# A one-layer hybrid encoder block on one core: residual update ahead of the last modulation tile, weight splits between operand pairs, roots read from PSUM, latent sums one block later, stores from two queues

## The reference

```
mod = silu(c) @ w_ada + b_ada          # six vectors: shift, scale, gate for mixer and MLP
h = rms_norm(x, norm_mix) * (1 + sc_a) + sh_a
p = h @ w_in                           # 3912 columns, split among three head groups
p_cq, p_ckv, p_kr, p_sb, p_fox, p_f = split(p)
q  = rms_norm(p_cq,  q_norm)  @ w_uq   # latent attention, group A
kv = rms_norm(p_ckv, kv_norm) @ w_ukv
o  = [mla(q, kv, rope(p_kr)), stick_breaking(p_sb), forgetting(p_fox, p_f)], per-head RMSNorm
x = x + g_a * (o @ w_out)
h = rms_norm(x, norm_ffn) * (1 + sc_m) + sh_m
x = x + g_m * (relu(h @ w_ff1) ** 2 @ w_ff2)      # d_ff = 8192
return rms_norm(x, final_norm)
```

## Time and profile before

| | |
|---|---|
| median of three runs | 1131.03 us (1129.48 to 1132.12) |
| the profiled execution, its own time | 1133.37 us |
| its span, first to last instruction | 1131.6 us |
| PE busy | 1098.3 us (97%) |
| DVE, ACT, POOL busy | 719.9, 532.8, 315.1 us |
| mean granted TensorE clock | 0.990 |
| read from HBM | 293.37 MB |

### The profile page before, as it was taken

How to read it: one execution, slowest core, us unless ns; L and a number is a source line. 1 busy time by engine, 2 the same in 40 slices (tenths; PEclk the granted TensorE clock), 3 DMA queues, 4 the chain that set the end, 5 groups by cost and what they waited for, 6 DMA issues and landing times.

```text
span 1131.6 us, 21714 instructions
## 1 busy us (share of the span) xinstructions
PE 1098.3 (97%) x9084; PEld 1065.4 (94%) x9084; DVE 719.9 (64%) x924; ACT 532.8 (47%) x674; POOL 315.1 (28%) x157
## 2 busy tenths in 40 slices
PE   7989999999999999999999999999999999999996
PEld 6879999997799989999999999999999999999995
DVE  4588877888866569877875544545655555444453
ACT  4644454676574445444444434334444544344341
POOL 2998997865049950000000000000000000000001
PEclk8999999999999999999999999999999999999998
DMA  9999999999759858888886665656566656565651
GB/s 348 409 409 403 398 372 371 379 352 330 248 226 408 326 204 314 307 302 284 279 272 195 190 202 189 197 192 191 183 206 196 193 191 201 190 196 189 193 184 75
DMA packets 81888, 296.88 MB, mean 262 GB/s; under 512 B 9088, under 2 KB 9216, under 8 KB 81792
## 3 DMA queue, kind: packets, MB, share of 16 engines
q1 hardware_dynamic: 81792, 295.50, 73.7%
HBM read 293.37 MB, written 2.10 MB: 261 GB/s over the span
## 4 chain that ended last, share of the span: by engine, by line
PE 83%; DMA 5%; DVE 3%; POOL 3%; issue 2%; ACT 1%; SPq 1%; DVEq 0%; ACTq 0%
PE ps L1408 50%; PE ps L1414 25%; DMA ada<-in_ada 3%; POOL w_lo L845 3%; PE ps L1426 2%; DMA raw<-in_weights 2%; PE ps L1595 2%; PE ps L1431 1%; DVE ada L972 1%; SPq L443 0%; POOL ssq L839 0%; PE ps L1605 0%; PE ps L1450 0%; ACT w_hi L493 0%; PE ps L1635 0%
## 5 line engine op out<-in xcount | busy, mean ns | idle before, releaser
L493 ACT ACTIVATE w_hi<-raw 128x1024 fp32r<-128x1024 f32 x338 | 355.3, 1059 | 431.4 <-PE ps L1414 358.2
L953 DVE TENSOR_TENSOR w_lo<-raw,w_hi 128x1024 fp32r<-128x1024 f32 x254 | 308.7, 1224 | 267.3 <-ACT w_hi L493 266.8
L1408 PE MATMUL ps<-hT,w_hi 128*128 128x256 f32 x3072 | 382.8, 277 | 8.3 <-DVEq L1040 3.0
L1408 PEld LDWEIGHTS ps<-hT,w_hi 128*128 128x128 f32 x3072 | 365.3, 189 | 12.0 <-issue 3.9
L1408 PE MATMUL ps<-act,w_hi 128*128 128x256 f32 x2048 | 252.9, 276 | 0.0
L1408 PEld LDWEIGHTS ps<-act,w_hi 128*128 128x128 f32 x2048 | 241.6, 188 | 0.0
L845 POOL TENSOR_TENSOR w_lo<-raw,w_hi 128x1024 fp32r<-128x1024 f32 x84 | 200.6, 2413 | 36.1 <-ACT w_hi L493 35.6
L1414 PE MATMUL ps<-hT,w_lo 128*128 128x256 f32 x1536 | 205.8, 276 | 0.7 <-DVE w_lo L953 0.7
L839 POOL TENSOR_TENSOR ssq<-ssq,sq 128x1024 f32<-128x1024 f32 x6 | 14.4, 2408 | 657.3 <-ACT sq L500 657.3
L1414 PEld LDWEIGHTS ps<-hT,w_lo 128*128 128x128 f32 x1536 | 188.8, 188 | 0.9 <-DVE w_lo L953 0.9
L1414 PE MATMUL ps<-act,w_lo 128*128 128x256 f32 x1024 | 136.9, 276 | 0.0
(11 more groups left out here) (229 smaller groups left out, 833.1 us busy)
## 6 DMA issues: line engine op xcount, KB each, us to landing
raw<-in_weights SPq DMA_DIRECT2D x338, 512.0 KB, 4.4
ada<-in_ada SPq DMA_DIRECT2D x176, 512.0 KB, 6.4
more<-in_weights SPq DMA_DIRECT2D x24, 512.0 KB, 7.6
more<-in_ada SPq DMA_DIRECT2D x16, 512.0 KB, 7.9
xT<-in_xt SPq DMA_DIRECT2D x4, 512.0 KB, 7.3
y<-tmp SPq DMA_DIRECT2D x4, 256.0 KB, 2.5
consts<-in_consts SPq DMA_DIRECT2D x1, 580.0 KB, 12.4
y<-sq SPq DMA_DIRECT2D x2, 256.0 KB, 3.0
```

What stands on the lines that cost most here:

```text
L493: sc.activation(w_hi[:, slot, :, :], raw_room(u0 + j), ACT.Copy).then_inc(hi_done, 1)
L953: ve.tensor_tensor(w_lo[:, slot, :, :], raw_room(u), w_hi[:, slot, :, :].bitcast(F32), ALU.subtract).then_inc(lo_vec, 1)
L1408: pe.matmul(acc[:, n, :], w, rhs[:, kt0 + k, half, :], start=first and k == 0 and n % 2 == 0 and half == 0, stop=False, skip_group_check=True)
```

## The change

Seven edits, in program order.

1. `USE_LST` goes from 37 to 38: PE makes the latents' sums after block 4 of the last part, and DVE's `latent_means` and ACT's `root_latents` move from block 4 to block 5. `lat_operand(1)` no longer follows `root_latents`; `lat_operand(2)` does.
2. DVE does `gate_out(3)` before `ada_tile(159)` and `make_gain`.
3. `rough` for the second norm and the final norm reads the sums in PSUM itself (Ln with scale 1/2048 and epsilon as a bias, a new column of `cols`). DVE's `mean` waits for that Ln, and so runs beside the Exp; `invert` waits for `mean` only at its second instruction.
4. The feed-forward's first unit (`first_unit`) multiplies the high operand half by all of `w_hi`, then `w_lo`, and only then the low half.
5. ACT converts B_FF+4 to B_FF+8 behind operand pairs 3 to 7; it was B_FF+4 and +5 behind pairs 6 and 7.
6. DVE splits B_FF+2 to B_FF+6 among the pairs (in passes 3, 4, 5, 7 and 8 of its loop); it was B_FF+2 and +3 in passes 3 and 4.
7. The three stores of POOL's results are issued by ACT, the five of DVE's by SP.

```
+            def rough(n, use=None, bank=0, ready=0):
+                if use is None:
...
+                else:
+                    sc.wait_ge(psum_ready, ready)
+                    sc.activation(y0[:, 0, :], ps[use % 2][:, bank, 0:S], ACT.Ln, scale=1.0 / D,
+                                  bias=cols[:, C_EPS:C_EPS + 1]).then_inc(ln_step, 1)
...
                 operand_hi(R_FFN + j, ...)
-                if j >= 6:
-                    hi(B_FF + LAG, 0, 0, j - 6)
+                if j >= 3:
+                    hi(B_FF + LAG, 0, 0, j - 3)
...
                 ve.wait_ge(newton, 2 * n - 5)
+                ve.wait_ge(mean_done, n)
...
-                    if last and b == 4:
+                    if last and b == 5:
                         latent_means()
...
-                    ada_tile(a)
+                    if a + 1 < A_GM:
+                        ada_tile(a)
...
+            gate_out(3)
+            ada_tile(A_GM - 1)
             make_gain(SC_M, C_FFN, 0, KT, A_GM - 1)
-            gate_out(3)
             ve.wait_ge(gain_ready, 9)
-            ve.wait_ge(psum_ready, READY_FFN)
+            ve.wait_ge(ln_step, 3)
...
-                if j in (3, 4):
-                    lo(B_FF + j - 1)
+                if j in (3, 4, 5, 7, 8):
+                    lo(B_FF + (3, 4, 5, 7, 8).index(j) + 2)
...
+            for n, k in enumerate((6, 8, 10)):
+                sc.wait_ge(result_pool, n + 1)
+                sc.dma_start(out[:, k * S:(k + 2) * S],
+                             result_tiles(k).rearrange("p a b -> p (a b)")).then_inc(ld_out, 16)
...
-            def unit(u, banks, rhs, kt0, ready, first, last, ahead=None):
+            def first_unit(u, banks):
+                acc = quarters(banks)
+                pe.wait_ge(hi_done, u + 1)
+                for k in range(UK):
+                    pe.wait_ge(*((first_hi, 1), (op_hi, R_FFN + 1))[k])
+                    for n in range(4):
+                        pe.matmul(acc[:, n, :], w_hi[:, u % RING, k, n * P:(n + 1) * P], hT[:, k, 0, :],
...
-                    if p + 1 == len(PARTS) and b == 3:
+                    if p + 1 == len(PARTS) and b == 4:
                         take(USE_LST)
```

More of the change, by code:

```diff
@@ L802, in _ @@
                     for b in range(2):
-                        for j in range(2 if half == it == b == 0 else 0, 8):
+                        for j in range(5 if half == it == b == 0 else 0, 8):
                             hi(base + LAG, 16, it, 8 * b + j)
@@ L1394, in take, with unit @@
                     pe.wait_ge(psum_free, use)
[L1396 removed]
+            def first_unit(u, banks):
[5 more added lines that the diff above has]
+                        pe.matmul(acc[:, n, :], w_hi[:, u % RING, k, n * P:(n + 1) * P], hT[:, k, 0, :],
+                                  start=k == 0 and n % 2 == 0, stop=False, skip_group_check=True)
+                pe.wait_ge(*lo_ready(u))
+                for k in range(UK):
+                    for n in range(4):
+                        pe.matmul(acc[:, n, :], w_lo[:, u % RING, k, n * P:(n + 1) * P], hT[:, k, 0, :],
+                                  start=False, stop=False, skip_group_check=True)
+                for k in range(UK):
+                    pe.wait_ge(*((first_lo, 1), (op_lo, R_FFN + 1))[k])
+                    for n in range(4):
+                        ins = pe.matmul(acc[:, n, :], w_hi[:, u % RING, k, n * P:(n + 1) * P], hT[:, k, 1, :],
+                                        start=False, stop=False, skip_group_check=True)
+                ins.then_inc(unit_used, 1)
+            def unit(u, banks, rhs, kt0, ready, first, last):
                 slot = u % RING
                 acc = quarters(banks)
[L1400 removed]
+                pe.wait_ge(*ready)
                 pe.wait_ge(hi_done, u + 1)
                 for k in range(UK):
[L1403 to L1404 removed]
                     for n in range(4):
```

39 lines of the change are left out of this document (17 added, 22 removed).

## The result

The changed kernel takes 1156.29 us, the median of four runs (1152.78 to 1157.76), against 1131.57 us (1129.48 to 1134.82, four runs) before: a ratio of 1.0212, interval 1.0189 to 1.0235. Forecast were 1124.4. The profiled execution took 1155.15 us, its span is 1153.4, the mean granted clock 0.992 (before 0.990).

A forecast was written before the change was run, and what follows sets the result against it. PE, busy 97% of the span, was taken to bound the kernel. Savings of 2.85 + 0.46 + 0 + 2.79 + 0 + 0.46 + 0.1 = 6.66 us took the median from 1131.03 to 1124.4 us, range 1122.4 to 1126.9.

The forecast's parts named there:

- Update ahead and root from PSUM: Passage into the feed-forward part: residual update first saves 2.85 us, Ln reading PSUM beside `mean` saves 0.46.
- The root term: Second norm's root: Ln reads PSUM at once, `mean` runs beside Exp; 0.46 us saved, bounds 0.46 gain, about 0.4 loss.
- First unit: Feed-forward unit 0: an earlier start only lengthens the stop before unit 1; 0 saved, bounds 0 and 0.1 us.
- Splits: Feed-forward unit 4: earlier splits remove PE's wait for `w_hi` and `w_lo`; 2.79 us saved, bounds 1.3 and 2.79.
- Rival (a): Feed-forward splits stay late: half of 2.79 us remains, 1125.8, or all, 1127.2; chance 0.11.
- Latents: Latents' sums after block 4: slow clock taken to come again, 0 saved; bounds 1.0 us saved, 0.7 lost.
- rival (e): Latents keep the full clock: 1.0 us saved and no slow-clock cost, 1123.4 or a little less; chance 0.05.
- rival (b): Clock falls at the feed-forward part's head, on units 0 to 2, costing 1.24 to 1.7 us: 1125.9; chance 0.06.
- Stores: Kernel's tail: two store queues fill part of the first transfer gap; 0.1 us saved, bounds 0.19 saved, 0.2 lost.

The follow-up runs named there:

- after: The changed kernel with all seven edits: 1156.29 us, median of four runs, ratio 1.0212 to the kernel before.
- a_old_first: Changed kernel with the old order of matmuls in the feed-forward's first unit: 1127.11, 1155.86, 1156.41 and 1157.08 us.
- b_early_splits: Kernel before with only the earlier conversions by ACT and splits by DVE: 1129.82, 1154.81, 1155.55 and 1163.16 us.
- a_late_splits: Changed kernel with the earlier conversions and splits undone: seven runs of 1128.38 to 1132.52 us, three of 1155.38 to 1158.98.
- before: The kernel without the change: 1131.57 us, median of four runs.
- b_set: Kernel before plus a float32 matmul ahead of feed-forward unit 6, an own-type one ahead of unit 10: eight runs 1129.96 to 1134.62 us, four 1159.17 to 1163.30.
- b_slow: Kernel before plus one float32 matmul ahead of feed-forward unit 6: 1132.0, 1157.1, 1160.83 and 1162.34 us.
- a_set: Changed kernel plus a float32 matmul ahead of feed-forward unit 2 and an own-type 128-column one ahead of unit 6: median 1128.45 us, six runs.
- a_own: Changed kernel plus only one own-type 128-column matmul ahead of feed-forward unit 6: 1127.29, 1129.26, 1154.21 and 1154.95 us.
- a_filler: Changed kernel plus a 128-column float32 matmul ahead of each of the 23 feed-forward blocks after the first: 1157.93 to 1159.73 us, four runs.
- the two probes: Changed kernel plus float32 matmuls ahead of every eighth feed-forward unit, with stops or matmuls of other kinds or widths between: 1160.57 and 1164.65 us.

## Why the prediction was wrong, step by step

**The step that failed** is the one that I gave no term: "16 matmuls in 1.81 us and 8 in 0.92 us, 2.73 us a unit, so a microsecond saved ahead of it arrives at the end whole." A unit is 2.72 or 2.83 us, and a stop of 2.8 us ahead of 250 units was the point that chose between them. The saving was 2.8, its price 27. That the two stops in unit 4 are such a point is shown; that the removal alone decides isn't, since without them a kernel ran F in two runs of 12. The evidence was in my rows: the last one of the earlier trace rows has 16 matmuls at 2.05 us. The four units from there, 201.14 to 212.45, run at S, and the granted clock was 1.00 over them. The prediction used only the start of that row.

How often each pace came: among kernels with no stop or disturbance between unit 1 and the end, 10 runs of 12 were slow (`after` 4 of 4, `a_old_first` and `b_early_splits` 3 of 4 each). With the stop before unit 4, the kernel before was slow in 9 of its 48 runs and `a_late_splits` in 3 of 10. That the removal of the stop is what shifts the odds is shown by the undone edits in both directions, by the two groups taken together more than by any pair of kernels: 10 of 12 against 12 of 58.

**Update ahead and root from PSUM, 2.85 + 0.46: the mechanism right, 3.06 between these two traces, but 1.5 to 2.4 in the other traces of the old order.** DVE and ACT of the changed kernel:

```profile
407.37 1.66 DVE L1055 SCALAR_TENSOR_TENSOR xT<-ps,mod,xT 128x256 f32<-128x256 f32 x4 [4.23 <-PE ps L1443]
...
410.60 0.17 DVE L1005 TENSOR_TENSOR gain<-mod,cols 128x16 f32<-128x16 f32 x1
411.40 0.42 DVE L985 TENSOR_SCALAR rstd<-ps 128x256 f32<-128x256 f32 x1 [0.62 <-ACT el L513]
411.98 0.43 DVE L992 SCALAR_TENSOR_TENSOR tmp<-el 128x256 f32<-128x256 f32 x1 [0.15 <-DVE rstd L985]
```

```profile
410.82 0.47 ACT L513 ACTIVATE el<-ps,cols 128x256 f32<-128x256 f32 x1 [0.40 <-PE ps L1479]
411.32 0.42 ACT L516 ACTIVATE el<-el 128x256 f32<-128x256 f32 x1
```

The update starts 0.20 after PE's sums (407.17), PSUM is ready 3.65 after them, as at the end of the kernel. So the new order does what was computed. What it is compared with isn't a constant: `b_early_splits`, `b_set` and `b_slow` have the code of before up to the root, and their traces say (us; the clock is that over the last eight sum matmuls):

| trace | first sum matmul to the root | POOL's splits end after it by | `gain` takes | clock |
|---|---|---|---|---|
| `before` | 9.20 | 2.95 | 2.35 | falls to 0.50 at 411.6 |
| `b_early_splits` | 8.51 | 2.72 | 3.01 | 1.00 |
| `b_set` | 7.78 | 1.99 | 1.48 | 1.00 |
| `b_slow` | 7.65 | 1.87 | 2.56 | 1.00 |
| the changed order, nine traces | 6.14 to 6.16 | | 0.17 to 0.18 | 1.00 |

The prediction held that none of its terms was peculiar to the traced execution. This one was: POOL was latest there, and only there did the clock fall before the sums were done. From the update's start to the root that trace takes 6.29 us and the other three 5.83, so 0.46 of the 2.85 was the slow clock. The Trainium skill (SBUF — State Buffer, on the shared port pair) says that the loser of the pair is blocked for the whole instruction and doesn't share; these traces agree: wherever `gain` starts beside POOL's splits (1.48 to 3.01 us) it ends within 0.05 us of them, and behind them it takes 0.17. The root term was 0.46 and measured 0.21: the Ln, which now reads PSUM and takes a bias from `cols`, takes 0.47, not 0.42 (inside my bounds; which of the two makes it longer no run tells), and `mean`, which starts 0.58 behind the Ln, ends after the Exp, so that `invert` waits for it, 0.15. At the end of the kernel `mean` starts 0.51 behind the Ln, `invert` follows at once, and the term measured 0.40 of 0.46.

**First unit, 0: right.** Unit 1 at root + 4.75, before 4.74.

**Splits, 2.79: right in size, and the cause of the loss.** No wait for `w_hi` or `w_lo` is left in the changed kernel. Rival (a) had named the thin spot, 0.15 us of slack at unit 5, and priced it one for one; `a_old_first` shows it 0.02 us short, followed by a loss of 27. In `a_set` the stretch from unit 1 is 1.95 us shorter than before; five units at S (0.53) and the two added matmuls put back (0.14 for the first, by the starts of unit 2 there and in `a_own`; the same taken for the second, an estimate), that is 2.76.

**Latents, 0: right within what the traces can tell, though the clock didn't do what I took it to.** I took it that the slow clock would come again. It didn't in `after` or in `a_set`, whose PE reads:

```profile
190.49 1.99 PE L1468 MATMUL ps<-w_hi,hT 128*128 128x512 f32 x8
...
199.53 2.10 PE L1450 MATMUL ps<-hT,w_hi 128*128 128x256 f32 x16 [0.28 <-DVEq L1047]
```

The stop before block 5 is 0.28, not 0.6, and from the start of block 3's last eight matmuls to block 5 it takes 9.95 us, where the trace of before takes 11.79. But the edit isn't what saved this. `b_early_splits` has the latents as they were, and its trace has neither the stop nor the slow clock:

```profile
188.68 1.07 PE L1415 MATMUL ps<-hT,w_lo 128*128 128x256 f32 x8
189.59 1.84 PE L1491 MATMUL ps<-cols,sq 128*128 128x1 f32 x16
...
198.21 1.99 PE L1409 MATMUL ps<-hT,w_hi 128*128 128x256 f32 x16
```

That is 9.54 us, and 9.56 in `b_set`; in `b_slow`, without the stop but with the clock at 0.50 from 193.1 to 196.5, 11.12. The ten traces with the edit take 9.38 to 10.64. In six of these the clock did fall, first between 198.1 and 203.2, in the sums or just behind them. So it fell around the sums in two of four traces in the old place and in six of ten in the new one; stretches of 200 to 202 in `a_set` and in `a_own`:

```profile
200.00:202.00 2.00, 2.00 (x20) 2.00 (x19) 1.16 (x1) 1.97 (x4) 2.00 (x2) 1.00 1.01 404
```

```profile
200.00:202.00 2.00, 2.00 (x12) 2.00 (x11) 1.25 (x3) 1.96 (x4) 2.00 (x2) 0.50 0.99 391
```

Whether the clock falls there differs from execution to execution, whatever the place of the sums, and why stays open: a stop ahead of the small matmuls isn't needed, as `b_slow` shows. What rival (e) described came true in `after`, but as luck of the execution. In the passage to the feed-forward part the clock fell in the trace of before alone, of all 14. With the change PE stood still there and the clock stayed at 1.00, so rival (b) fell.

**Stores, 0.1: nothing.** From the copy of the root to the end 8.44 before, 8.45 and 8.44 after. The Trainium skill (DMA: Bandwidth & Descriptors, "Issuing engines are not separate DMA queues") says that only issue time is saved, and these traces agree.

At equal pace the forecast's span comes out, by luck: the span of `a_set` is 1124.8, the forecast's 1124.9. The 6.80 us between it and the trace of before are 1.41 ahead of the sums, 3.06 at the root, 1.95 from unit 1 on, 0.39 at the last root, less 0.01. The 1.41 aren't the change's: `b_early_splits` and `b_slow` start the sums at 404.75 and 404.67, ahead of `a_set` at 404.88. And against the other three traces of the old order the 3.06 are 1.5 to 2.4. So the pair of traces shows more than the edits give, and `a_late_splits`, with 1.1 us saved of 3.87, says the same. By the medians `a_set` is 0.41% faster than before, 4.6 us (3.1 to 6.2), which the rest of the sum, 3.8 to 5.4, fits.

## What to carry to other kernels

A rhythm has to be measured before it is used as a constant: compare the matmul count of equal stretches, or the start-to-start time of a unit, across stretches and between traces, at the same granted clock, before anything upstream is priced at its face value. A long stream multiplies whatever its first matmuls settle; an edit that only removes a stop ahead of it can cost ten times the stop, and being a few hundredths of a microsecond late with what feeds it can cost far more than the time it is short. A saving that is read from one trace of the kernel before holds that execution's own bad luck (a slow clock, a late engine); a second trace of the same code shows which of it is the code's. Where a kernel's runs fall into two groups, look for the first place where their traces differ in pace, and judge an edit within each group before judging how it moves the odds.

## What the runs showed of the hardware

- Pairs of a weight load and a 256-column matmul run at 113.3 or 117.8 ns, both at a granted clock of 1.00, over hundreds of microseconds, with PE busy 100% either way. The difference is 4%, 27 us in this kernel.
- In the feed-forward part of all 14 traces the pace changed only at a stop, at a matmul of another kind or width, or at a weight load 18 ns late (`a_old_first`), and then lasted up to 250 units. A single matmul of 0.13 us turned the pace: to slow in `a_filler` and `b_slow`, with one of another kind to fast in `a_set`; over 250 units that is 27 us.
- In the two probes, behind the float32 matmul, one of the stream's own width changed nothing (8 of 8) and 64, 128 and 384 columns turned slow to fast (24 of 24). Stops of 1.21 us at the head of a unit changed nothing (8 of 8), shorter ones did (8 of 8).
- A weight load that waits for a split of VectorE starts 51 to 54 ns after the split's end (five traces).
- The granted clock fell to 0.50 for 3 to 7 us in or just behind the latents' sums in 8 of 14 traces, at either place of the sums, and not in the other six.
